# Second modulation of a two-block transformer kernel: products with the silu vector moved from TensorE to GpSimd

## The reference

```python
mod = (jax.nn.silu(c.astype(F32)) @ ada_w.astype(F32) + ada_b.astype(F32)).astype(x.dtype)
sh1, sc1, g1, sh2, sc2, g2 = [m[:, None, :] for m in jnp.split(mod, 6, axis=-1)]
h = rms_norm_2(x, norm1_g) * (1 + sc1) + sh1
```

## Time and profile before

| | us |
|---|---|
| median of three executions (least, greatest) | 2445.43 (2443.59, 2448.99) |
| profiled execution, from its first to its last instruction | 2452.4 |
| PE busy with matmuls, share of the span | 91% |
| DVE busy | 48% |
| ACT busy | 19% |
| POOL busy | 16% |

### The profile page before, as it was taken

One profiled execution on the slowest core, in us unless ns is written; L12 is line 12 of the kernel. 1 busy time (PEld: TensorE's weight loads), 2 busy tenths in 40 slices (PEclk: granted clock), 3 DMA queues, 4 the chain that ended last, 5 costly groups with the idle time before them and its releaser, 6 DMA issues. The chain is left out here.

```text
span 2452.4 us, 25630 instructions
## 1 busy us (share of the span) xinstructions
PE 2227.1 (91%) x9579; PEld 1099.4 (45%) x9579; DVE 1166.9 (48%) x2231; ACT 458.1 (19%) x894; POOL 396.4 (16%) x771
## 2 busy tenths in 40 slices
PE   6998988999998999999987999988879999999975
PEld 3444654443443446444344488635433333333322
DVE  3447853222222031000896533423876667677755
ACT  2013561111111011000425433101001111111111
POOL 0005000400000000000100000000054444444533
PEclk9999999999999999999988999988989999999988
DMA  9412000545424104981302100302099999899976
GB/s 372 192 57 78 35 1 35 207 164 192 175 76 156 69 4 156 386 311 57 107 18 93 61 7 3 138 34 86 1 368 389 415 379 391 351 421 384 378 287 249
DMA packets 68557, 446.46 MB, mean 182 GB/s; under 512 B 12228, under 2 KB 12884, under 8 KB 43506
## 3 DMA queue, kind: packets, MB, share of 16 engines
q0 software_dynamic: 36176, 254.42, 26.0%
q1 hardware_dynamic: 32290, 190.78, 20.2%
HBM read 416.27 MB, written 73.45 MB: 200 GB/s over the span
## 5 line engine op out<-in xcount | busy, mean ns | idle before, releaser
L2594 PE MATMUL psum<-arena 128*64 128x512 f32 (+1 forms) x1088 | 366.9, 604 | 38.4 <-DVE arena L2642 16.4
L2642 DVE STREAM_TRANSPOSE arena<-arena 32x256 f32<-32x256 f32 x832 | 362.1, 435 | 15.6 <-DMA arena<-scratch_h,arena 3.9
L969 PE MATMUL psum<-arena 128*128 128x512 f32 x704 | 307.4, 596 | 3.2 <-PEq L901 3.2
L2594 PEld LDWEIGHTS psum<-arena 128*64 128x64 f32 (+1 forms) x1088 | 144.0, 166 | 226.3 <-issue 201.6
L969 PEld LDWEIGHTS psum<-arena 128*128 128x128 f32 x704 | 133.3, 191 | 177.5 <-issue 177.5
L2585 PE MATMUL psum<-arena 128*64 128x512 f32 (+1 forms) x544 | 186.2, 598 | 1.1 <-ACT arena L2620 1.1
L1028 DVE SCALAR_TENSOR_TENSOR arena<-psum,arena 128x511 f32<-128x511 f32 x88 | 66.0, 750 | 253.9 <-ACT arena L1003 252.4
L1099 PE MATMUL psum<-arena 128*128 128x512 f32 x352 | 153.6, 598 | 7.0 <-PEq L157 7.0
L864 PE MATMUL psum<-arena 128*128 128x512 f32 x256 | 113.3, 603 | 8.7 <-DMA arena<-in_w_out 7.9
L2585 PEld LDWEIGHTS psum<-arena 128*64 128x64 f32 (+1 forms) x544 | 68.5, 163 | 113.1 <-issue 111.8
L1228 PE MATMUL psum<-arena 128*128 128x512 f32 x256 | 110.0, 592 | 0.0
(11 more groups left out here) (509 smaller groups left out, 2935.1 us busy)
## 6 DMA issues: line engine op xcount, KB each, us to landing
scratch_expert_out<-arena SPq DMA_DIRECT2D x18, 2048.0 KB, 18.1
scratch_expert_out<-arena SPq DMA_DIRECT2D x51, 512.0 KB, 10.0
arena<-in_w_ada SPq DMA_DIRECT2D x12, 2048.0 KB, 17.0
arena<-in_ada_w POOLq DMA_DIRECT2D x12, 2048.0 KB, 8.0
arena<-in_w_up SPq DMA_DIRECT2D x22, 1024.0 KB, 4.8
arena<-in_w_in SPq DMA_DIRECT2D x9, 2048.0 KB, 8.6
arena<-in_w_down SPq DMA_DIRECT2D x5, 2048.0 KB, 7.7
arena<-in_w_o SPq DMA_DIRECT2D x2, 2048.0 KB, 8.5
```

The costliest lines, as they stand in the source:

```text
L969: last = pe.matmul(K.bank[2 * (n % 3) + half], w[:, k, P * half:P * half + P], K.h[:, k, :], start=(k == 0), stop=(k == KD - 1))
L2594: last = pe.matmul(K.bank[2 + s][r, :], xt[:, s, P * k + r.start:P * k + r.stop], gu[:, lane, 2 * E_FF * k:2 * E_FF * (k + 1)], start=(k = ...
L2642: last = dve.transpose(channels[c:c + 32, :, a:a + 32], tokens[a:a + 32, :, c:c + 32])
```

## The change

The eight product matmuls and ACT's copy are taken out. POOL does the products itself: each block of the tile is multiplied in place by its partition's element of the silu vector (128x512, eight instructions without waits between them), and the eight blocks are added in halves, 4 + 4, 2 + 2, 1 + 1, the last add writing `K.part`. PE only sums `K.part` over all 128 partitions, now with columns of `K.ones` in place of the selectors. POOL waits for its tile to land and for PE to have read the half of `K.part` that it writes. It issues tile j + 2 after the adds of tile j. The signals `a2mm` and `a2copy` are replaced by `weighed` and `a2sum`.

```diff
@@ PE, ada_end @@
-                pe.wait_ge(a2copy.sem, j + 1)
+                pe.wait_ge(a2sum.sem, j + 1)
                 if j < 4:
-                    a2cols.by(ada_columns(pe, K.bank[7], K.part[:, j % 2, :], K.sel[:, :], j))
+                    a2cols.by(ada_columns(pe, K.bank[7], K.part[:, j % 2, :], K.ones[:, 0:2], j))
                 else:
                     if j > 4:
                         pe.wait_ge(a2out.sem, j - 3)
-                    a2rows.by(pe.matmul(K.bank[7], K.sel_rows[:, :], K.part[:, j % 2, :], start=True, stop=True))
+                    a2rows.by(pe.matmul(K.bank[7], K.ones[:, :], K.part[:, j % 2, :], start=True, stop=True))
@@ PE, loop over n @@
-                if 0 <= j < ADA_TILES:
-                    pe.wait_ge(a2in[j % 2].sem, 16 * (j // 2 + 1))
-                    pe.wait_ge(a2copy.sem, j)
-                    a2mm.by(ada_products(pe, K.bank[6], aw[:, j % 2, :], K.vec2))
@@ ACT, loop over n @@
-                j = n - FIRST
-                if 0 <= j < ADA_TILES:
-                    act.wait_ge(a2mm.sem, j + 1)
-                    if 2 <= j < 6:
-                        act.wait_ge(a2cols.sem, j - 1)
-                    if j >= 6:
-                        act.wait_ge(a2rows.sem, j - 5)
-                    a2copy.by(act.activation(K.part[:, j % 2, :], K.bank[6], ACT.Copy))
@@ POOL @@
             def ada(j):
                 if j >= 2:
-                    pool.wait_ge(a2mm.sem, j - 1)
+                    pool.wait_ge(a2sum.sem, j - 1)
                 a2in[j % 2].by(pool.dma_start(aw[:, j % 2, :], d["ada_w_2"][j]), 16)
...
-            for j in range(2, ADA_TILES):
-                ada(j)
-            pool.wait_ge(a2mm.sem, ADA_TILES)
+            for j in range(ADA_TILES):
+                pool.wait_ge(a2in[j % 2].sem, 16 * (j // 2 + 1))
+                if 2 <= j < 6:
+                    pool.wait_ge(a2cols.sem, j - 1)
+                if j >= 6:
+                    pool.wait_ge(a2rows.sem, j - 5)
+                tile = aw[:, j % 2, :]
+                for k in range(KD):
+                    w = tile[:, 512 * k:512 * k + 512]
+                    weighed.by(pool.tensor_scalar(w, w, K.vec2[:, k, 0:1], None, ALU.mult))
+                pool.wait_ge(weighed.sem, weighed.n)
+                link(pool, pool.tensor_tensor(tile[:, 0:2048], tile[:, 0:2048], tile[:, 2048:4096], ALU.add), weighed)
+                link(pool, pool.tensor_tensor(tile[:, 0:1024], tile[:, 0:1024], tile[:, 1024:2048], ALU.add), weighed)
+                link(pool, pool.tensor_tensor(K.part[:, j % 2, :], tile[:, 0:512], tile[:, 512:1024], ALU.add), a2sum)
+                if j + 2 < ADA_TILES:
+                    ada(j + 2)
             n2in.by(pool.dma_start(aw[:, 0, 0:D], d["norm2_g"].partition_broadcast(P)), 16)
```

More of the change, by code:

```diff
@@ L946, in phase_ffn_up @@
     a2bias, n2in = K.dma_signal("ada2_bias"), K.dma_signal("norm2_g_landed")
-    a2mm, a2copy, a2cols, a2rows, a2out = (sig(n) for n in ("ada2_used", "ada2_copied", "ada2_columns", "ada2_rows", "ada2_rows_out"))
+    weighed, a2sum, a2cols, a2rows, a2out = (sig(n) for n in ("ada2_weighed", "ada2_summed", "ada2_columns", "ada2_rows", "ada2_rows_out"))
     col_bank = K.bank[7][:, 0:32].rearrange("p (m v) -> p m v", v=2)
```

## The result

The changed kernel is slower: 2503.0 us (median of four; 2501.5 to 2505.1) against 2447.2 us of before in the same runs (2443.6 to 2453.2), a ratio of 1.022 with a 95% interval of 1.021 to 1.024. Forecast was 2423.1 us, with a range of 2417 to 2438.

A forecast was written before the change was run, and what follows sets the result against it. PE, busy 91% and gapless in the phase, was taken as the bound. Twelve tiles of product matmuls, 22.3 us, come off and nothing is put on: 2445.4 - 22.3 = 2423.1 us, range 2417 to 2438.

The forecast's parts named there:

- the price of the products: POOL's multiply of a 128x512 block: 0.60 us each, eight 4.8 us a tile; upper bound 1.19 each, 9.5.
- POOL becomes the bound: Rival, chance 0.08: products at 1.19 us make P 18.9, tile 11 comes 6.3 us late, total 2453 us.
- P free up to 16.5 us: POOL's time per tile may reach 16.5 us at no cost; beyond, each extra microsecond costs 12.
- the stall: PE's 3.3 us wait for DVE's L1036 ahead of the first row matmul, iteration 9; forecast to stay.
- The lock: Rival, chance 0.07: at P 15.3 to 17.3, L1036 begins inside POOL's long add; stall up to 4.7 us more, 2428 to 2433.
- What PE loses, 22.3 us: Product matmuls L245 leave PE's list in the second modulation: twelve tiles at 1.86 us, 22.3 us off.
- The period: PE's time from one modulation tile to the next in the up-projection: 16.57 us before, 14.71 without the products.
- Adds, transfers, ACT: POOL's adds cost 8.2 us a tile; transfers stay hidden, landing in 8.0, at worst 12.6; ACT's lost copies gain nothing.
- One term: POOL's gaps where a linked instruction waits for the one before: four of 0.08 us each, 0.3 a tile.
- POOL against DVE: Two-SBUF-input DVE products and POOL instructions delay each other; most L1021 pairs delayed but covered, some 0.65 us every second tile.
- the spare of iteration 9: POOL's idle margin before DVE's L1036 starts at 575.7: 2.9 us at P of 14.2, gone at 15.3.
- What follows the phase is only moved.: Stages behind the edited phase's common end (780.18) only start earlier, so the phase's 22.3 us reach the total.

The follow-up runs named there:

- one multiply: Changed kernel with one two-input multiply of 4096 elements, silu vector broadcast, in place of each tile's eight products; 2435.6 us against 2452.5 of before, ratio 0.993.
- two operations: Changed kernel with an added 0.0 as second operation in each product, computing the same; 2430.1 us against 2445.1 of before, ratio 0.9935.
- without products: Changed kernel without the eight products of each tile, adds kept, modulation left unweighted; 2434.2 us against 2452.5 of before, ratio 0.9935.
- the single instructions: Changed kernel with a row of single linked POOL multiplies in several forms put behind the last tile; 2499.9 us in its one execution.

## Why the prediction was wrong

**The step that failed** is the price of the products. The prediction took 0.60 us, by the line through POOL's one-input rows (COPY, and `tensor_scalar` of L795), and kept 1.19 as upper bound, because "only one tensor is read". Measured: 1.555, so a tile costs POOL 7.6 us more in products alone. The line was drawn through instructions of another form. L795 multiplies and adds; the change only multiplies, and POOL is slower at less. The bound did not bound either: I took the two-input rate for the worst that an elementwise instruction can do. The number of operations in an instruction was never on my list of what might matter.

**The rival that came true** is the prediction's own second one: POOL becomes the bound. Its mechanism and its arithmetic were right, its size was not, because it ended at P = 18.9 (P is POOL's time for a tile). With the measured P of 21.9, tile 11 is ready at 483.0 + 12 x 21.9 = 745.8; PE summed it at 747.5, in a trace that began the phase 0.6 us later. That is 44 us behind before. Some 2 us more are the stretched L969 behind it (70.94 us for 68.83). The slow clock behind the ten stalls (PEclk is 0.88 over the stretch from 528.4 to 747.5) added little more: PE had time to spare there, since POOL set the pace.

**P free up to 16.5 us.** Not borne out. At 21.3 and 21.9 PE waits for a tile, and at 16.6 (one multiply for all eight) it does not, but at 16.6 the phase is 5.8 us longer than at 14.9 (332.4 against 326.6). PE did not wait for a tile only because it had been held up itself, by 3.0 us more at iteration 9 and by a lower clock at the phase's start (0.78 for 0.89 over the first 14 us) and behind the stall (0.50 for 0.62 over the first 4.5 us). POOL's last add and PE's last row sum with one multiply, then PE's last row sum with two operations:

```profile
681.26 1.27 POOL L1071 TENSOR_TENSOR arena<-arena 128x512 f32<-128x512 f32 x1
684.44 1.02 PE L961 MATMUL psum<-arena 128*128 128x512 f32 x2
```
```profile
677.32 1.02 PE L961 MATMUL psum<-arena 128*128 128x512 f32 x2
```

With two operations PE is there 249.9 us after the phase's start (427.38). With one multiply (start 428.79) that would be 678.7, and the tile was ready at 682.5. The lock and the limit of 16.5 were written down as two separate things; the lock comes first.

**What PE loses, 22.3 us.** Right in mechanism, 24.1 measured without products and 24.2 with two operations. The period, 14.71 forecast, is 14.6 us. Two neighbouring column sums and two row sums with two operations, then two row sums of before:

```profile
526.02 0.95 PE L252 MATMUL psum<-arena 128*128 128x2 f32 x8
540.64 0.95 PE L252 MATMUL psum<-arena 128*128 128x2 f32 x8
...
604.36 1.02 PE L961 MATMUL psum<-arena 128*128 128x512 f32 x2
618.95 1.02 PE L961 MATMUL psum<-arena 128*128 128x512 f32 x2
```
```profile
620.25 1.02 PE L961 MATMUL psum<-arena 128*128 128x512 f32 x2
636.89 1.02 PE L961 MATMUL psum<-arena 128*128 128x512 f32 x2
```

So a tile gives back some 2.0 us and not 1.86 (with rows 16.64 - 14.59): the sum beside the products gets shorter as well. The two levels of the clock show in the trace of before: behind the stall it is 0.50 in each half microsecond from 586.5 to 589.5 and 1.00 from 589.8 to 603; of 20400 windows of 0.1 us across the trace 18978 have 1.00 and 1382 have 0.50.

**Adds, transfers, ACT.** Right: 8.1 us for 8.2, no wait for a tile. One term was too small: POOL's transfer issue begins 0.56 us after the add that it waits for, not 0.08, 0.5 us more a tile than counted.

**POOL against DVE.** The mechanism was right, the place as well, and with two operations the longest DVE product took 5.0 us, as forecast. That figure and the lock rival's price of 4.7 us were the author's estimate: both take the whole add for the delay, and no row of before shows more than the 0.8 us by which L1021 was late. The runs showed 3.0 us (L1023 with one multiply, 3.14 for 0.17) and 4.3 us (a product at 611.80 with two operations, 5.00 for 0.69, beside the add from 611.42 to 616.25). In the changed kernel L1023 began at 593.38 and took 0.73 us in place of 0.17, held up to the end of an add (592.82 + 1.26 = 594.08), so the spare of iteration 9 was gone, as the prediction said it would be at this P. The spare was overrated, though. With two operations, P at 14.9 and 15.9 by turns, the 2.9 us of spare were down to nothing (572.97 against 572.95), and that the stall stayed at 3.3 us was luck.

**"What follows the phase is only moved."** Wrong by about 9 us. In the changed kernel the phase lost 397.5 - 350.8 = 46.7 us and the total 55.8. In the traces 6 to 8 of these 9 us stand behind the phase (1672.7 against 1665.1 and 1666.4).

Had the products been written with two operations, the total would have been 2430 (as measured), inside the range of 2417 to 2438, but 7 us above the forecast, for that last reason.

## What to carry to other kernels

A price taken from another line is a price of that line's exact form: compare operand kinds, number of inputs and number of operations before drawing a line through it. If no row has the form, a bound from "the slowest kind I know" is no bound; where a break-even is near (here P = 18.4 against an estimate of 14.2), the slack counts for less than the least certain factor, here one that is multiplied by 96. A limit worked out for one wait (P up to 16.5) holds only while no nearer one, here the one of DVE behind a POOL add, at 15.3, moves the others. And time taken out of one phase need not arrive whole at the end: here 24 us brought 15 to 18.

## What the runs showed of the hardware

- GpSimd's `tensor_scalar` on float32, 512 elements a partition: 1.49 us (constant) and 1.56 us (value per partition) with one operation, a multiply; 0.62 to 0.71 us with multiply and add (kernel with the single instructions). At 2048 elements with one operation 5.44 us, which is more than the 4.51 us of an add of two tensors (two operations, L1071).
- GpSimd's two-input multiply with a broadcast second operand took less than an add of two tensors: 4096 elements in 7.03 us, 1.7 ns each, where 2048 elements of the add take 4.51 us, 2.2 ns each (the same two kernels).
- A DVE `tensor_scalar` of eight elements took 3.14 us (0.17 with two operations) while GpSimd was inside a 4.5 us add, though it had nothing to do with the add's data (one multiply, L1023). An equally small DVE instruction with one input in PSUM took 0.17 us beside the same add (L1022).
- The same 160 matmul records of a stage without any edit took 38.39 or 40.06 us, at a mean granted clock of 0.88 (third trace of before) or 0.87 (second trace with two operations); in 16 traces the stage's two lengths, 57 and 58.6 us, sort by when it starts.
